# The first recurrence with its stages in another order, values turned without their mean, and token halves swapped in two of four tiles

## The reference, cut to what matters

```python
def step(S, inp):
    r_t, w_t, k_t, v_t, a_t, b_t = inp
    sa = jnp.einsum('bhvk,bhk->bhv', S, a_t)
    S = S * w_t[:, :, None, :] + sa[..., None] * b_t[:, :, None, :] + v_t[..., None] * k_t[:, :, None, :]
    return S, jnp.einsum('bhvk,bhk->bhv', S, r_t)
...
mu = jnp.mean(y, -1, keepdims=True)
var = jnp.mean(jnp.square(y - mu), -1, keepdims=True)
y = ((y - mu) * lax.rsqrt(var + RWKV_GN_EPS)).reshape(B, T, RWKV_DIM) * lnx_g + lnx_b
bonus = jnp.sum(r * k * r_k, -1, keepdims=True) * v
y = y + bonus.reshape(B, T, RWKV_DIM)
return y * g
```

## Time and profile before

| What | Value |
|---|---|
| Median of 3 timed runs | 2222.52 us (2221.08 to 2222.68) |
| Span of the profiled execution | 2220.0 us |
| Time of that execution beside its span | not listed; 2.5 us lie between span and median |
| Mean granted TensorE clock | 0.989 of full |
| PE, PEld, DVE, ACT busy | 2123.2, 1692.3, 1241.2, 822.4 us |
| The `rwkv` block in the trace | about 221.8 to 345.3 us |
| of it setup, levels, recurrence | 34.5, 40.3, 48.7 us |

### The profile page before, as it was taken

The page is one execution under the profiler, slowest core; times in us unless marked ns, Lnnn a source line. Parts: engine busy times, 40 slices in busy tenths (PEclk is TensorE's granted clock), DMA queues, the critical chain, the costliest instruction groups (busy, mean ns, idle before and its releaser), DMA issues. The chain is left out here.

```text
span 2220.0 us, 30690 instructions
## 1 busy us (share of the span) xinstructions
PE 2123.2 (96%) x12558; PEld 1692.3 (76%) x12558; DVE 1241.2 (56%) x1704; ACT 822.4 (37%) x1294; POOL 262.7 (12%) x268
## 2 busy tenths in 40 slices
PE   8899999999999989999999999999998899999996
PEld 6776987778887778888777788877665578878875
DVE  5546866642343476676573444458768737534544
ACT  4344323631232334444352322335234544222321
POOL 0000002000001100000110890020652010000002
PEclk9999999999999999999999999999999999999998
DMA  6120002222322222222132222324211042223221
GB/s 227 67 67 29 3 4 86 85 95 96 102 98 76 76 86 76 67 76 67 48 95 95 91 95 96 102 81 130 67 57 34 2 142 86 93 88 112 96 71 64
DMA packets 51675, 179.23 MB, mean 81 GB/s; under 512 B 5784, under 2 KB 5784, under 8 KB 51280
## 3 DMA queue, kind: packets, MB, share of 16 engines
q1 hardware_dynamic: 47712, 165.45, 23.0%
q10 hardware_dynamic: 3328, 8.13, 1.0%
q0 software_dynamic: 496, 3.69, 0.4%
HBM read 172.51 MB, written 4.21 MB: 80 GB/s over the span
## 5 line engine op out<-in xcount | busy, mean ns | idle before, releaser
L1132 DVE TENSOR_TENSOR w_lo<-w_raw,w_hi 128x1024 fp32r<-128x1024 f32 (+1 forms) x320 | 412.4, 1290 | 730.6 <-ACT w_hi L1125 730.4
L1230 PE MATMUL banks<-xh,w_hi 128*128 128x512 f32 x1560 | 624.6, 400 | 4.6 <-PEq L213 3.6
L1232 PE MATMUL banks<-xh,w_lo 128*128 128x512 f32 x1560 | 609.8, 391 | 0.0
L1231 PE MATMUL banks<-xl,w_hi 128*128 128x512 f32 x1560 | 609.2, 391 | 0.0
L1125 ACT ACTIVATE w_hi<-w_raw 128x1024 fp32r<-128x1024 f32 (+1 forms) x320 | 328.6, 1029 | 722.0 <-PE banks L1232 685.3
L1230 PEld LDWEIGHTS banks<-xh,w_hi 128*128 128x128 f32 x1560 | 294.3, 189 | 83.6 <-issue 20.5
L1232 PEld LDWEIGHTS banks<-xh,w_lo 128*128 128x128 f32 x1560 | 293.6, 188 | 62.9
L1231 PEld LDWEIGHTS banks<-xl,w_hi 128*128 128x128 f32 x1560 | 294.2, 189 | 58.9 <-issue 1.7
L1230 PE MATMUL banks<-hh,w_hi 128*128 128x512 f32 x688 | 271.9, 395 | 11.7 <-DVE w_lo L1132 4.8
L1232 PE MATMUL banks<-hh,w_lo 128*128 128x512 f32 x688 | 269.2, 391 | 0.0
L1231 PE MATMUL banks<-hl,w_hi 128*128 128x512 f32 x688 | 269.1, 391 | 0.0
(11 more groups left out here) (509 smaller groups left out, 2669.7 us busy)
## 6 DMA issues: line engine op xcount, KB each, us to landing
w_raw<-in_w SPq DMA_DIRECT2D x128, 512.0 KB, 3.4
w_raw<-in_w_gu SPq DMA_DIRECT2D x44, 512.0 KB, 3.4
w_raw<-in_w_c_in SPq DMA_DIRECT2D x40, 512.0 KB, 3.4
w_raw<-in_w_ab_in SPq DMA_DIRECT2D x27, 512.0 KB, 3.5
w_raw<-in_w_in SPq DMA_DIRECT2D x25, 512.0 KB, 3.5
w_raw<-in_w_down SPq DMA_DIRECT2D x16, 384.0 KB, 3.0
w_raw<-in_w_down SPq DMA_DIRECT2D x16, 320.0 KB, 2.8
w_raw<-in_w_ab_out SPq DMA_DIRECT2D x8, 512.0 KB, 3.4
```

The lines of the kernel that those rows point to most:

```text
L1132: dve.tensor_tensor(lo[:, 0:n], core.raw[u % RAW][:, 0:n], hi[:, 0:n].bitcast(F32), ALU.subtract).then_inc(core.split_ready, 1)
L1230: pe.matmul(bank, hi[:, w], src.xh[:, kk, :], start=kk == 0, stop=False)
L1231: pe.matmul(bank, hi[:, w], src.xl[:, kk, :], start=False, stop=False)
L1232: mm = pe.matmul(bank, lo[:, w], src.xh[:, kk, :], start=False, stop=last)
```

## The change

It does six things to this block and to the load ahead of it:

- `at`, `elast` and `rt` are formed on DVE in the load block (j == 26) and no longer at the start of `rwkv`.
- In tiles 1 and 3 whatever has tokens on its partitions lies on the other half (`timed`). A product that goes from features to tokens or back then reads one half and writes the other in these tiles, while products of tokens with tokens stay on one half. Consecutive pairs of products go to two PSUM banks (`b`).
- The block-diagonal operands are gone. `pair` takes the products inside a chunk with 64 by 64 weights and 128 moving columns; `group` took 128 by 128 weights. Turns and products alternate, v is turned last, and ACT copies two tiles at once (8 copies of 1024 columns in place of 16 of 512).
- v is turned by the identity less 1/64, so that the values lose their mean over a head. The outputs then have none, and `mean` and `centre` are gone.
- `XT`·`Aak` is formed for all chunks ahead of the recurrence (`xd_ready`), ACT copies it, and DVE adds it to the state's part when it forms `SA`; before, PE added it in PSUM and ACT copied `SA`.
- PE's list of the recurrence is written out in another order, the outputs of a chunk are formed one chunk late, and the normalisation runs over two chunks at a time.

```diff
+        if j == 26:
+            at, rt = self.AR[:, :, :, 0, :], self.AR[:, :, :, 1, :]
+            chunked = lambda ap: ap.rearrange("p c (n t) -> p c n t", t=C)
+            dve.wait_ge(s.e_before, 4)
+            dve.wait_ge(s.scaled, 2)
+            dve.scalar_tensor_tensor(at, chunked(kk), -1.0, at, ALU.mult, ALU.mult).then_inc(s.asked, 1)
+            dve.wait_ge(s.e_in, 4)
+            dve.wait_ge(s.rk_sum, 4)
+            dve.tensor_copy(self.elast, rt[:, :, :, C - 1]).then_inc(s.last_kept, 1)
+            dve.wait_ge(s.last_kept, 1)
+            dve.tensor_tensor(rt, rt, chunked(self.r), ALU.mult).then_inc(s.received, 1)
...
-    heads = [(c, e) for c in range(4) for e in range(2)]
...
+    timed = lambda c, e: half(e ^ (c % 2))
+    heads = [(2 * q + b, q, b, e) for q in range(2) for b in range(2) for e in range(2)]
...
-        diag = [st.sb(f"diag{i}", [P, NCH, P]) for i in range(2)]
...
+        TOK = [("b", 0), ("k", 0), ("a", 0), ("b", 1), ("k", 1), ("a", 1), ("v", 0), ("v", 1)]
...
+            for i, (what, c) in enumerate(TOK):
+                act.wait_ge(s.tok, i + 1)
+                act.activation(TOK_OUT[what][:, 2 * c:2 * c + 2], core.banks[:, TOK_BANKS[i % 2], :].rearrange("p b (n t) -> p b n t", t=C),
+                               ACT.Copy).then_inc(s.tok_out, 1)
...
+            def told(n):
+                dve.wait_ge(s.sa_ready, n)
+                dve.tensor_tensor(paired(SAs[:, n % 2]), two_banks(SA_BANKS), of_chunk(Aak, n), ALU.add).then_inc(s.sa_out, 1)
...
-            def centre(n):
-                dve.wait_ge(s.mean, n + 1)
-                dve.scalar_tensor_tensor(at[:, :, n], quarters(core.psum[4]), -1.0 / 64, at[:, :, n], ALU.mult, ALU.add).then_inc(s.centred, 1)
...
+            def pair(p, of, a_, h):
+                banks = PAIR_BANK[p % 2]
+                if p == 1:
+                    pe.wait_ge(s.bonus_ready, 1)
+                if p > 1:
+                    pe.wait_ge(s.masked, 2 * (p - 1))
+                for m in range(4):
+                    for b in range(2):
+                        c, n = 2 * a_ + b, 4 * h + m
...
-                def group(diag_, rhs, out, ready, sem):
-                    pe.wait_ge(ready, 2 * c + 2)
-                    for n in range(NCH):
-                        mm = pe.matmul(out(n), diag_[:, n, :], rhs(n), start=True, stop=True)
-                    mm.then_inc(sem, 1)
...
+                            mm = pe.matmul(core.psum[banks[b]][timed(c, e), m * P:(m + 1) * P], of[half(e), c, n],
+                                           AR[half(e), c, n].rearrange("p a t -> p (a t)"), start=True, stop=True)
+                mm.then_inc(s.pairs, 1)
+
+            def tok(i):
...
                 for n in range(NCH):
-                    for e in range(2):
...
+                    for b in range(2):
+                        c = 2 * a_ + b
+                        for e in range(2):
+                            turn = centred[half(e)] if what == "v" else ident[half(e), 64 * e:64 * e + 64]
+                            mm = pe.matmul(core.psum[banks[b]][timed(c, e), n * C:(n + 1) * C], src[half(e), c, n], turn, start=True, stop=True)
+                mm.then_inc(s.tok, 1)
...
-            def mean(n):
-                pe.wait_ge(s.y_out, n + 1)
...
+                    mm = pe.matmul(core.psum[XD_BANKS[g]][rows_, of_bank(b, m)], XT[rows_, a_, h, b, m], Aak[rows_, a_, h, b, m], start=True, stop=True)
+                mm.then_inc(s.xd_ready, 1)
...
+            def told(n):
+
+                pe.wait_ge(s.a_out, n)
+                pe.wait_ge(s.h_out, n)
+                for c, q, b, e in heads:
+                    mm = pe.matmul(core.psum[b][timed(c, e), q * C:(q + 1) * C], at[half(e), c, n], states[half(e), n % 2, c], start=True, stop=True)
+                mm.then_inc(s.sa_ready, 1)
...
+            def state_values(n):
+                for c, q, b, e in heads:
+                    pe.matmul(core.psum[H_BANK[b]][half(e), q * C:(q + 1) * C], tokK[timed(c, e), c, n], tokV[timed(c, e), c, n],
+                              start=q == 0, stop=False, skip_group_check=True)
+
+            def state_answers(n):
+                pe.wait_ge(*((s.sa_out, n) if n else (s.xd_out, 3)))
+                for c, q, b, e in heads:
+                    mm = pe.matmul(core.psum[H_BANK[b]][half(e), q * C:(q + 1) * C], tokB[timed(c, e), c, n], answers(n, c, e),
+                                   start=False, stop=True, skip_group_check=True)
...
+            def y_states(n):
+                pe.wait_ge(s.start_ready, n)
+                if n < NCH - 1:
+                    pe.wait_ge(s.y_out, n)
+                for c, q, b, e in heads:
+                    mm = pe.matmul(y_at(n, q, b, e), starts[half(e), n % 2, c], rt[half(e), c, n], start=q == 0, stop=False, skip_group_check=True)
...
+            def y_values(n):
                 if n:
-                    pe.wait_ge(s.centred, n)
-                pe.matmul(quarters(core.psum[4]), core.const("blk"), at[:, :, n], start=True, stop=True).then_inc(s.mean, 1)
-
...
+            def y_answers(n):
+                for c, q, b, e in heads:
+                    mm = pe.matmul(y_at(n, q, b, e), answers(n, c, e), of_head(Arb, c, e, n), start=False, stop=True, skip_group_check=True)
                 mm.then_inc(s.y_ready, 1)
...
+            pe.wait_ge(s.a_out, 6)
+            asked((7,), Q_BANK)
+            for n in range(3, NCH - 1):
+                told(n)
+                y_states(n - 1)
+                state_values(n)
+                state_answers(n)
+                if n % 2:
+                    pe.wait_ge(s.a_out, 7)
+                    var((n - 3) // 2)
+                y_values(n - 1)
+                y_answers(n - 1)
```

More of the change, by code:

```diff
@@ L1437, in _ @@
-                if n:
-                    logs(n - 1)
-            square(NCH - 1)
-            logs(NCH - 1)
+                answer(n)
+                if n in (2, 4, 6):
+                    logs(n // 2 - 1)
+                square(n)
+                if n == 2:
+                    for c in range(4):
+                        act.wait_ge(s.gated, c + 1)
+                        act.activation(gate[:, c, :], gate[:, c, :], ACT.Copy, scale=core.param("gng", c)).then_inc(s.gate_scaled, 1)
+            logs(3)
@@ new lines, in _ @@
+            question(1)
+            question(2)
+            state(0)
+            start(1)
+            question(3)
+            question(4)
+            told(1)
+            gated(0)
+            state(1)
+            start(2)
+            told(2)
+            question(5)
+            question(6)
+            state(2)
+            start(3)
+            gated(1)
+            told(3)
+            question(7)
+            gated(2)
+            state(3)
+            start(4)
+            gated(3)
@@ L1541, in _ @@
+            told(4)
+            finish(0, 0)
+            state(4)
+            start(5)
+            told(5)
+            finish(0, 1)
+            state(5)
+            start(6)
+            finish(0, 2)
+            told(6)
+            finish(1, 0)
+            state(6)
+            start(7)
+            told(7)
+            for i, steps in ((1, (1, 2)), (2, (0, 1, 2)), (3, (0, 1, 2)), (4, (0, 1, 2))):
+                for step in steps:
+                    finish(i, step)
         @block.tensor
@@ new lines, in var @@
+            def var(i):
+                pe.wait_ge(s.squared, DONE[i])
+                if i:
+                    pe.wait_ge(s.log, i)
+                n = len(SPANS[i])
+                rhs = squares[:] if n == 2 else squares[:, 256 * (i % 2):256 * (i % 2) + 256]
+                pe.matmul(core.psum[VAR_BANK][:, 0:4 * C * n], core.const("blk"), rhs, start=True, stop=True).then_inc(s.var, 1)
+            asked((1, 2), Q_BANK)
+            state_values(0)
+            pe.wait_ge(s.xd_out, 4)
+            asked((3, 4), Y_BANK)
@@ L1690 @@
+            told(7)
+            y_states(6)
+            y_states(7)
+            y_values(6)
+            y_answers(6)
+            y_values(7)
+            pe.wait_ge(s.sa_out, 7)
+            y_answers(7)
+            var(2)
+            var(3)
+            keep_busy(core, pe, 7, 1)
+            var(4)
+            keep_busy(core, pe, 7, 4)
 HALF_ROWS = (slice(0, 64), slice(64, 128))
```

491 lines of the change are left out of this document (232 added, 259 removed).

## The result

The changed kernel takes 2208.0 us (median of 4 runs, 2205.7 to 2210.8) against 2221.8 (4 runs, 2218.6 to 2222.7) measured beside it: 0.9942 of the time before, with a 95% interval of 0.9930 to 0.9955. Its repeat (e13) gave 0.9935 (0.9920 to 0.9951). So it is 13.8 us faster, half of the 27 that were forecast. The profiled execution took 2210.8, its span is 2209.0, 11.0 less than that of before.

What follows compares the result with a forecast made beforehand. PE's records times their price were taken to bound the block, wherever DVE does not take over. Savings of 13.2 us before the recurrence and 14.5 in it, 27.7 off the 2220.0 span, gave 2192.3, as median 2195; 0.8 in 2188 to 2213.

Steps and rivals of the forecast that it cites:

- the likeliest case: Whole kernel: four squares of the array work at once, giving 2195 us, own range 2189 to 2201, chance 0.62.
- The price of a record across squares: Turns and `pair` on PE: with four squares at work, 14.6 ns a 64-column record and 28 ns a `pair` record.
- So PE's count of records times their price is the block's time, wherever DVE does not take over: Whole block: PE's records times their price set its time, except where DVE is the bound; turns cost 29.2 ns before.
- one record per 29 ns from ahead of the array: Rival, chance 0.14: something ahead of the array hands out a record every 29 ns, so turns gain nothing; time 2206.
- two at a time: Rival, chance 0.16: squares off the diagonal gain nothing, 29.2 ns for 64 columns and 56 for `pair`; time 2212.
- Setup: Block start to levels: PE 16.5 us, DVE the bound with 20.15; levels start at 20.9 against 34.5, 13.6 saved.
- Levels "nothing": Levels: DVE at 1.92 us a step stays the bound, so nothing is gained or lost.
- Lead-in: Start of the recurrence, from DVE's last sum of the levels to `told(3)`: 10.4 us.
- Chunks: Chunks 3 to 6 of the recurrence: about 2.5 us each plus waits on DVE and ACT, 12.7 us in all.
- End: End of the recurrence, from `told(7)` and the last outputs through the last idle matmuls: 10.7 us.
- Late start: Load block: three instructions added on DVE make the block start 0.4 us late.
- The clock under 1 in the block: Sign of a wrong forecast: granted clock under 1 in the block, as PE pauses up to 1.5 us more often.

Runs made afterwards that it cites:

- e13: The changed kernel measured once more, with nothing altered: 2206.9 us, 0.9935 of the kernel before.
- e1: The changed kernel with both heads of every tile on their own halves again, none crossing to the other half: 2217.5 us, 0.9977 of the kernel before.
- e10: The changed kernel with the products of `XT` and `Aak` at the recurrence's start in half as many records, each of 128 columns: 2203.3 us (0.9904).
- e11: The changed kernel with four idle records of 512 columns on TensorE at the end of the load block: 2204.1 us (0.9917).
- e12: The changed kernel with every head on its own half and the first turn made nine times, over two squares: 2234.2 us (1.0053).
- e4: The changed kernel with the first of each level's two products in half as many records, each of 128 columns: 2201.3 us (0.9907).
- e5: The changed kernel with its first turn, 64 records over four squares, made nine times instead of once: 2223.4 us (1.0010).
- e6: The changed kernel with turns of b, k and a that go to the first half made as transpositions, alternating with products: 2224.8 us (1.0012).

## Why the prediction was half right

The measured 2208 lies inside the stated range of 2188 to 2213, but only because that range took in rivals; the likeliest case had 2195 and its own range of 2189 to 2201. Its condition, four squares at work, held, and its time did not.

*The price of a record across squares* (14.6 ns; `pair` 28): right, 14.8 and 27.

*"So PE's count of records times their price is the block's time, wherever DVE does not take over"*: this is the step that failed. Besides the array and VectorE there is a third bound, the delivery of instructions, 128 records with their weight loads in 3.45 us or more. At 29.2 ns a record the kernel before lay just under it and never showed it. The PE sum of 16.5 us up to the levels has 832 records, which are 6.5 packets, 22.4 us at 3.45; PE started the levels at 24.0 us (246.76 less 222.77), where the forecast had 20.9.

*Rival "one record per 29 ns from ahead of the array"* (0.14): the nearest of all. It gave a time of 2206, in part by luck: it had PE start the levels at 25.8 (24.0 measured) and the recurrence gain 7.8 (9.56 measured), and it had no loss in the levels or behind the block. My argument against it, starts in pairs, shows that bursts exist and says nothing on a mean. Its mechanism was not quite this either: not each record is held back, but each 128th.

*Rival "two at a time"* (0.16): it was not the case here, and e1 bears out its setup. Its 40.5 us for the recurrence do not follow from the terms beside it: 10.4, four chunks of 3.48, 2.7 of waits and 10.7 make 37.7. e1 has 41.49 to ScalarE's next block.

*Setup:* DVE as the bound, wrong as a consequence; it waited 5.34 us for PE and came to its first L1494 after 25.89 us instead of 22. Its own work, 19.9 us, was right (20.15).

*Levels "nothing"*: mis-sized by 1.75, the gaps at every 256th instruction. Why packets come in time in the kernel before and in e1 (39.2 us), but late in the changed kernel, its repeat, e10 and e11 (40.7 to 42.4), is open: an emptied store at their start is not the whole answer, since e12 entered them from an unstarved setup and took 41.4.

*Lead-in* (10.4): 14.85, of which 3.84 are issue pauses; e10 shows 10.75 once 64 records are out of the way. *Chunks* (12.7): 13.7 to 15.1, 12.95 without the gate's work. *End* (10.7): right. *Late start* (0.4): 0.96, of which some 0.65 was there before the added instructions (VectorE starts L449 at 216.98 instead of 216.32).

*The clock under 1 in the block*, which I named as a sign that would make me wrong: it came, and cost the setup nothing that was seen. Far behind the block a fall of the clock cost 5 us of that one execution.

Forecast less measured is 16.7 us in the profile: setup 3.9, levels 1.75, recurrence 4.9, start 0.56, rest 5.6. Without the last, 27.7 becomes some 16.6, of which the medians show 13.8 and 15.3.

## What to carry to other kernels

Count instructions as well as columns: when TensorE's small records average near 27 to 30 ns, halving their array time gains little, and fewer, wider records gain more (e4, e10). A pause marked issue that returns after the same number of instructions is a sign of it; look at the instruction queue's packets. Before making a stage faster by some resource, check how close the next bound already lies; here it was 7 per cent away, unseen in any wait.

## What was not expected of the hardware

TensorE's instructions arrive in packets of 16 KB; under full demand 128 records with their loads in 3.45 us (e5), since the next packet starts only 1.13 us after the one before is taken up, and PE goes on 2.33 us after that start. After a quieter stretch a burst of 274 records went at 17 to 18 ns before the first pause. At a granted clock of 0.50, turns over four squares took 26.6 ns, at 1.00 14.8. Transpositions and products in turn took 0.43 us for six records at full clock, and 0.66 at half (e6); grouped, 48 records took 1.59 us.
